# Rows of rounded products on a cleared array, issued on TensorE ahead of the first tile of a hybrid convolution, attention and PEER block

## The chip, the cores and the metric

The kernel runs on one core of one Trainium2 chip. Its time is device microseconds of that core for one execution: 997.12 us, the median of two runs (997.07 and 997.18).

## What is computed

The reference is one layer of a causal decoder block over 256 tokens of 1,024 channels, all in float32:

```
h = x + W_out( sig(g_conv) * ConformerConv(xn) + sig(g_attn) * DilatedAttn(xn) ),  xn = RMSNorm(x)
y = h + PEER(RMSNorm(h))
```

One input projection of `xn` gives the input of the convolution, the queries, keys and values of 12 heads of 64 in three dilation groups, and two gates. `PEER` scores product keys (8 heads, 2 x 128 sub-keys, the best 16), and then sums over 16,384 single-neuron experts: their activations are `gelu(u_e . x)` times a softmax gate, and the output is the sum of `act * v_e`. None of this is touched by the change: the products that it adds read an array of zeros and constants, and nobody reads what they write.

## The kernel before, in words

Weights come from HBM as tiles of 128 x 1,024 float32 (512 KB). The first 76 (`N_FRONT`) are the projections, then come 128 tiles of `u` and 128 of `v`. `raw`, `hi` and `lo` are rings of four slots. SyncE queues the loads (`load`, L387), each as soon as the slot of `raw` is free, which is when `lo` of the tile four back is made. ScalarE rounds a tile to float32r (`split_hi`, L335), which waits until TensorE is done with the slot of `hi`. GpSimd or VectorE computes the rest, raw minus hi (`split_lo`, L354). TensorE multiplies in three rounded products, hi x hi, hi x lo and lo x hi, for each block of 128 x 128 weights (`product`, L1218 for the input and `u` tiles, 256 columns each; L1527 and L1553 for the `v` tiles, 512 columns each). "Rounded product" below means such a float32r matmul; it is one instruction of the profile. A matmul on float32 operands stands in the profile as two instructions (the 27 warm-ups as 54), a float32 transpose as one.

The order on TensorE is a list written by hand (`jobs_in_order`), each job with a bank of PSUM and the waits for what it reads. It starts with 27 warm-up matmuls (`WARM_UP`, L1233: 128 columns of ones, float32, into bank 5), which wait only for `ones` (`const` at 2). Then it waits for `const` at 7 and goes to `first_tiles` (L1242 in `high_products`, L1249 in `low_products`, L1265 for the sums of squares), which work on the input before its norm is known. Their operands come from ScalarE (`xg_hi` at L481, `hi` at L335) and VectorE (`xg_lo` in `x_lo` at L738, and L748). The sums of squares are needed by ScalarE's square root, that by VectorE's reciprocal, and that by the normalised input in `norm_space`, which is first written after this point. So `norm_space` is unused until then.

`norm_space` holds 4,104 float32r values on each partition. The moving operand of a rounded product in the input stage begins 8 values (32 bytes) behind its start (`SHIFT`). Other kinds of work between the rounded products, which the prediction uses: `bias_row` (L1228), the sums over heads (L1286, two columns of `kmask`, and L1296), transposes (L1440, L1491, L1495), the gate products in float16 (L1476), and `spread_k` (L1306), which waits for VectorE's `rk_parts`.

GpSimd makes the constants at the start: `ones`, `ident`, `u_pad`, `kmask` (L434 to L440), and an affine select that puts ones on the diagonal of `ident` (L442), which takes `const` to 8.

Of the kernel before, what the change touches and what calls it, by code (L numbers as in the profile page):

```python
# [7 lines left out]
F32 = mybir.dt.float32  # L8
F32R = mybir.dt.float32r
U32 = mybir.dt.uint32  # L10
F16 = mybir.dt.float16
# [4 lines left out]
P = 128  # L16
D = 1024
T = 256
# [33 lines left out]
PICK_TILE = 60  # L52
HALF = NK // 2
GATE_SCALE = 2.0 ** 15
WARM_UP = 27
G_SHARED = N_FRONT + HALF + LEAD
TOK = 8
PAIR = 2
# [107 lines left out]
def hybrid_block(nc, x_t, front, cols, rel_bias, onehot, sub_keys, u_tiles, v_tiles, out):  # L166
    bias_row = nc.dram_tensor("bias_row", (HEADS, BW), F32, kind="Internal").ap()
    toeplitz = nc.dram_tensor("toeplitz", (HEADS, P * BW), F32, kind="Internal").ap()
    with ExitStack() as ctx:
        def sb(name, shape, dt=F32, stack=ctx):  # L170
            return stack.enter_context(nc.sbuf_tensor(name, shape, dt))

        def sem(name):
            return ctx.enter_context(nc.semaphore(name))

        bank = [ctx.enter_context(nc.psum_tensor(f"bank{i}", [P, 512], F32)) for i in range(8)]


        norm_space = sb("norm_space", [P, KB * 2 * T + SHIFT], F32R)
# [4 lines left out]
        ident = sb("ident", [P, P])  # L184
# [4 lines left out]
        def tmp(name, shape, dt=F32):  # L189
            return sb(name, shape, dt, inner)  # L190

        ones = tmp("ones", [P, P])
# [3 lines left out]
        kmask = tmp("kmask", [P, 2 * HEADS - 2])  # L196
# [77 lines left out]
        pe_step = sem("pe_step")  # L274
        act_evac, dve_evac = sem("act_evac"), sem("dve_evac")
        const = sem("const")
        squared = sem("squared")
        pair_sums = sem("pair_sums")
        normed = sem("normed")
# [422 lines left out]
        def _(dve):  # L702
# [31 lines left out]
            def x_lo(k):  # L734
# [4 lines left out]
                                         in1=xg_hi[:, i, :].bitcast(F32), op0=ALU.mult, op1=ALU.subtract)\  # L739
                   .then_inc(xlo, 1)  # L740

            dve.wait_ge(gain_in, 16)
            for k in range(XG_ACT):
                if k % 4 == 0:
# [343 lines left out]
            weights = [21] * HALVES + [25] + TC * ([13] + [35] * (PH // 2) + [25] + [13, 18, 12] * 2 + [3])  # L1088
# [109 lines left out]
        def _(pe):  # L1198
# [32 lines left out]
            pe.wait_ge(const, 2)  # L1231
            for _ in range(WARM_UP):
                pe.matmul(bank[5][:, 0:P], ones[:, :], ones[:, :], start=True, stop=True)  # L1233
            pe.wait_ge(const, 7)

            def high_products(b, n):
# [171 lines left out]
            for b_ in range(KB):  # L1408
                b = start(("attn", b_))
                units = list(range(AB * b_, AB * b_ + AB))  # L1410
                for u in units:
                    n = T_ATT + u // 8
                    if b_ == 0:
                        freed(pe, ("o", u))
                    ins = product(b[:, 0:T], n % RING, [(u % 8, u % AB)], o_hi, o_lo, n, 0, 0,
                                  first=u == units[0], last=u == units[-1])
# [16 lines left out]
            for u in range(2, HALVES):  # L1433
                step(full(T_WQ + u, ("wq", u), xg_hi, xg_lo))
                if u == 2:

                    freed(pe, ("mix", KB - 1))
                    for c in range(TC):
                        for k in range(KB):
                            ins = pe.matmul(bank[2 * c + k // 4][:, (k % 4) * P:(k % 4 + 1) * P],  # L1440
                                            resid[:, k, c * P:(c + 1) * P], ident[:, :], is_transpose=True,
                                            start=k % 4 == 0, stop=False, skip_group_check=True)
# [3 lines left out]
            for j in range(N_SC):  # L1446
                b = start(("sc", j))
                for r in range(4):
# [3 lines left out]
                                    start=r == 0, stop=True, skip_group_check=True)  # L1452
# [93 lines left out]
            for b in range(4):  # L1546
                c, cols = b // 2, slice(b % 2 * 512, b % 2 * 512 + 512)
                for j in (RING - 2, RING - 1):
# [3 lines left out]
                    for a_, v_ in ((act_hi, hi), (act_hi, lo), (act_lo, hi)):  # L1552
                        ins = pe.matmul(bank[b][:, :], a_[:, j, c * P:(c + 1) * P], v_[:, j, cols],  # L1553
                                        start=False, stop=j == RING - 1 and a_ is act_lo, skip_group_check=True)
# [73 lines left out]
```

## Time and profile before

| | us |
|---|---|
| median of two runs | 997.12 |
| the profiled execution, as timed | 997.07 |
| its span in the profile | 995.2 |
| outside the span | 1.9 |
| TensorE matmuls busy | 989.8 |
| VectorE busy | 774.9 |
| ScalarE busy | 506.8 |
| GpSimd busy | 465.3 |

Times are microseconds from the start of the span. PE is TensorE, PEld its weight loads, DVE VectorE, ACT ScalarE, POOL GpSimd, and SPq the queue of SyncE. A matmul's duration in the trace covers its way through a pipeline, and several are under way at once. What one costs in a row of many is the distance from its start to the next start, so the prediction works with starts, or with a stretch divided by its count. In a row of the windows view, "(x20)" counts each matmul that is under way somewhere in the window, so some two or three that began before it are in the count. The granted clock is a share of full speed.

### The profile page before, as it was taken

The numbers are of one execution on the slowest core, as the hardware profiler recorded it, in microseconds if no ns is written. First come the engines' busy times: TensorE is split into PE (matmuls) and PEld (weight loads), VectorE is DVE, ScalarE is ACT, GpSimd is POOL, SyncE is SP. The second block draws the span as 40 slices with busy tenths as digits, with TensorE's granted clock in tenths as the row PEclk, the third lists the DMA queues.
The fourth block names the chain that finished last, engine by engine and source line by source line (L and its number), as shares of the span: only waits on it lengthen the run. The fifth ranks groups of instructions, "written<-read, shape, count | busy, mean of one in ns | idle before, by whom it ended". The sixth has DMA issues, their size and how long they took to land.

```text
span 995.2 us, 21854 instructions
## 1 busy us (share of the span) xinstructions
PE 989.8 (99%) x7822; PEld 917.0 (92%) x7822; DVE 774.9 (78%) x1304; ACT 506.8 (51%) x789; POOL 465.3 (47%) x198
## 2 busy tenths in 40 slices
PE   9999999999999999999999999999999999999998
PEld 9998999999999999999999999888888888888887
DVE  5999784868899996097777777988888876776764
ACT  6663877544555544544444444444444445554443
POOL 3664366656689999874444444100000004344442
PEclk9999999999999999999999999999999999999999
DMA  6684445654455565555555555555554555556562
GB/s 242 211 308 150 149 148 162 212 201 149 150 197 200 171 211 188 191 176 184 177 180 174 182 172 169 185 175 170 177 180 171 182 174 190 190 189 195 186 203 90
DMA packets 52619, 181.95 MB, mean 183 GB/s; under 512 B 5943, under 2 KB 9155, under 8 KB 52452
## 3 DMA queue, kind: packets, MB, share of 16 engines
q1 hardware_dynamic: 52292, 181.16, 54.4%
q8 instruction: 25, 0.41, 0.2%
q10 hardware_dynamic: 288, 0.27, 0.1%
q14 instruction: 14, 0.11, 0.0%
HBM read 180.33 MB, written 3.43 MB: 185 GB/s over the span
## 4 chain that ended last, share of the span: by engine, by line
PE 93%; DVE 5%; ACT 1%; issue 0%; POOL 0%; ACTq 0%; DVEq 0%; POOLq 0%
PE bank L1218 50%; PE bank L1527 35%; DVE bank L798 3%; PE bank L1476 3%; PE bank L1319 1%; PE bank L1233 1%; PE bank L1451 1%; DVE lo L354 1%; PE bank L1242 1%; PE bank L1553 1%; PE bank L1335 1%; ACT hi L335 0%; PE bank L1358 0%; PE bank L1346 0%; PE bank L1249 0%
## 5 line engine op out<-in xcount | busy, mean ns | idle before, releaser
L354 POOL TENSOR_TENSOR lo<-raw,hi 128x1024 fp32r<-128x1024 f32 x184 | 462.4, 2527 | 515.9 <-ACT hi L335 515.4
L335 ACT CAST hi<-raw 128x1024 fp32r<-128x1024 f32 x332 | 348.0, 1049 | 218.0 <-PE bank L1527 186.3
L1218 PE MATMUL bank<-norm_space,hi 128*128 128x256 f32 x2624 | 452.4, 278 | 0.2 <-POOL lo L354 0.2
L1218 PEld LDWEIGHTS bank<-norm_space,hi 128*128 128x128 f32 x2624 | 396.2, 188 | 1.8 <-issue 1.2
L1218 PE MATMUL bank<-norm_space,lo 128*128 128x256 f32 x1312 | 362.8, 277 | 0.0
L1527 PE MATMUL bank<-hi,norm_space 128*128 128x512 f32 x1008 | 273.8, 391 | 0.0
L1218 PEld LDWEIGHTS bank<-norm_space,lo 128*128 128x128 f32 x1312 | 246.4, 188 | 0.0
L1527 PEld LDWEIGHTS bank<-hi,norm_space 128*128 128x128 f32 x1008 | 188.0, 188 | 38.5
L354 DVE TENSOR_TENSOR lo<-raw,hi 128x1024 fp32r<-128x1024 f32 x148 | 189.2, 1279 | 27.4 <-ACT hi L335 27.3
L1527 PE MATMUL bank<-lo,norm_space 128*128 128x512 f32 x504 | 155.5, 390 | 0.0
L1145 DVE TENSOR_TENSOR norm_space<-act,norm_space 128x256 fp32r<-128x256 f32 x128 | 111.7, 876 | 48.8 <-ACT norm_space L665 48.8
L645 ACT ACTIVATE act<-bank 128x256 f32 (+1 forms) x128 | 49.2, 384 | 187.8 <-PE bank L1218 187.8
L1527 PEld LDWEIGHTS bank<-lo,norm_space 128*128 128x128 f32 x504 | 94.6, 188 | 19.7
L1218 PE MATMUL bank<-rounded_space,hi 128*128 128x256 f32 x496 | 87.0, 280 | 0.0
L1138 DVE SCALAR_TENSOR_TENSOR act<-bank,act 128x512 f32 (+1 forms) x64 | 41.4, 686 | 51.7 <-PE bank L1476 51.7
L1126 DVE TENSOR_TENSOR ohB<-eqB,parts 128x1024 f16<-128x1024 f16 x64 | 81.4, 1272 | 0.0
L1218 PEld LDWEIGHTS bank<-rounded_space,hi 128*128 128x128 f32 x496 | 75.4, 188 | 0.9 <-issue 0.6
L1218 PE MATMUL bank<-rounded_space,lo 128*128 128x256 f32 x248 | 69.1, 278 | 0.0
L665 ACT CAST norm_space<-act 128x256 fp32r (+1 forms) x128 | 51.4, 402 | 0.1
L1218 PEld LDWEIGHTS bank<-rounded_space,lo 128*128 128x128 f32 x248 | 47.0, 190 | 0.0
L798 DVE SCALAR_TENSOR_TENSOR bank<-u_pad,prm,bank 128x256 f32<-128x256 f32 x116 | 46.3, 481 | 0.0
L1122 DVE TENSOR_TENSOR ohA<-iota_nk,keys 128x1024 f16<-128x1024 f16 x64 | 46.1, 720 | 0.0
(183 smaller groups left out, 651.5 us busy)
## 6 DMA issues: line engine op xcount, KB each, us to landing
raw<-u_tiles SPq DMA_DIRECT2D x128, 512.0 KB, 3.3
raw<-v_tiles SPq DMA_DIRECT2D x128, 512.0 KB, 3.3
raw<-front SPq DMA_DIRECT2D x76, 512.0 KB, 3.8
toeplitz<-bias_row SPq DMA_DIRECT2D x6, 384.0 KB, 7.5
bias<-toeplitz SPq DMA_DIRECT2D x12, 128.0 KB, 3.5
resid<-x_t SPq DMA_DIRECT2D x2, 512.0 KB, 4.7
qk<-sub_keys SPq DMA_DIRECT2D x1, 1024.0 KB, 8.0
y<-act SPq DMA_DIRECT2D x3, 256.0 KB, 2.0
```

Source lines behind the costliest of these rows:

```text
L335: act_e.copy(hi[:, s, :], raw[:, s, :]).then_inc(hi_ready, 1)
L354: eng.tensor_tensor(lo[:, s, :], raw[:, s, :], hi[:, s, :].bitcast(F32), ALU.subtract)\
L645: a.activation(act[:, it * 4 + (base_i + j), :], bank[4 + j % 2][:, 0:T], ACT.Gelu).then_inc(gelu_done, 1)
L665: a.copy(act_hi[:, (base_i + j) % RING, :], act[:, it * 4 + (base_i + j), :]).then_inc(a_hi, 1)
L798: dve.scalar_tensor_tensor(out=acc[:, b, :] if w == TAPS - 1 else part_sum, in0=src, scalar=wt, in1=part_sum, op0=ALU.mult, op1=ALU.add).t ...
L1122: dve.tensor_tensor(ohA[:, g % 2], every_pair(iota_nk[:, :, :], NK), at(keys[:, 0, t], NK), ALU.is_equal).then_inc(spread, 1)
L1126: dve.tensor_tensor(ohB[:, g % 2].rearrange("p a i n b -> p (a i) n b"), eqB[:, :, :, :].unsqueeze(2).broadcast_to([P, TOK // PAIR, 2, HAL ...
L1138: dve.scalar_tensor_tensor(out=av, in0=gv, scalar=1.0 / GATE_SCALE, in1=av, op0=ALU.mult, op1=ALU.mult)\
L1145: dve.tensor_tensor(act_lo[:, s, :], act[:, it * 4 + (base_i + j), :], act_hi[:, s, :].bitcast(F32), ALU.subtract).then_inc(a_lo, 1)
L1218: ins = pe.matmul(dst, w_[:, s, u * P:(u + 1) * P], x_[:, k, :], start=first and i == 0 and p_ == 0, stop=last and i == n - 1 and p_ == 2)
L1476: ins = pe.matmul(bank[6 + g][:, q * HALF:(q + 1) * HALF], ohA[:, g, q // PAIR, :, q % PAIR], ohB[:, g, q // PAIR, i, :, q % PAIR], start= ...
L1527: ins = pe.matmul(bank[2 * c + half][:, :], a_[:, j, c * P:(c + 1) * P], v_[:, j, half * 512:(half + 1) * 512], start=False, stop=False, s ...
```

## The change

`WARM_UP` goes from 27 to 20. VectorE clears the first 6 x 256 values of `norm_space` before anything else. Behind the warm-ups TensorE waits for that and for `const` at 8. Then it issues rows of rounded products that read both operands from the cleared part, all into bank 5:

- for each of eight pairs of positions (`LAYOUTS`), three times: two instances of another kind (transposes, float32 products with two columns, float32 products with 128 columns), then 11 rounded products of 256 columns;
- for each of 14 kinds of interruption: two transposes, 10 rounded products, the interruption (rounded products of other widths or positions, float16 products with 64 columns, a float32 product), 9 rounded products.

That makes 264 and 266 rounded products of 256 columns, 44 transposes, and 10 further rounded products, 11 float16 products, 17 float32 products of 128 columns and 17 of two.

```
-WARM_UP = 27
+WARM_UP = 20
+LAYOUTS = ((8, 448), (8, 192), (24, 448), (24, 192), (0, 448), (0, 192), (16, 448), (16, 192))
...
+        cleared = sem("cleared")
...
+            dve.memset(norm_space[:, 0:6 * T].bitcast(F32), 0.0).then_inc(cleared, 1)
             dve.wait_ge(gain_in, 16)
...
             for _ in range(WARM_UP):
                 pe.matmul(bank[5][:, 0:P], ones[:, :], ones[:, :], start=True, stop=True)
+            pe.wait_ge(cleared, 1)
+            pe.wait_ge(const, 8)
+
+            def rounded_products(first, apart, count, columns=T, weights=P):
+                at = first + 4 * T - apart // 4
+                for _ in range(count):
+                    pe.matmul(bank[5][0:weights, 0:columns], norm_space[:, at:at + weights],
+                              norm_space[:, first:first + columns], start=True, stop=True)
+
+            def turned(count):
+                for _ in range(count):
+                    pe.transpose(bank[5][:, 0:P], ones[:, :], ident[:, :])
+
+            def masks(count):
+                for _ in range(count):
+                    pe.matmul(bank[5][:, 0:2], ones[:, :], kmask[:, 0:2], start=True, stop=True)
+
+            def full_products(count):
+                for _ in range(count):
+                    pe.matmul(bank[5][:, 0:P], ones[:, :], ones[:, :], start=True, stop=True)
+
+            def half_products(count):
+                narrow = norm_space[:, 0:P].bitcast(F16)
+                for _ in range(count):
+                    pe.matmul(bank[5][:, 0:64], narrow[:, 0:P], narrow[:, P:P + 64], start=True, stop=True)
+
+            for first, apart in LAYOUTS:
+                for before in (turned, masks, full_products):
+                    before(2)
+                    rounded_products(first, apart, 11)
+
+            between = (lambda: rounded_products(8, 448, 1, 64), lambda: rounded_products(8, 448, 1, 128),
+                       lambda: rounded_products(8, 448, 1, 32), lambda: rounded_products(8, 448, 1, 224),
+                       lambda: rounded_products(8, 448, 1, 240), lambda: rounded_products(8, 448, 2, 128),
+                       lambda: rounded_products(8, 416, 1), lambda: rounded_products(8, 416, 1, 64),
+                       lambda: rounded_products(8, 448, 1, 512), lambda: half_products(1), lambda: half_products(2),
+                       lambda: half_products(8), lambda: full_products(1), lambda: masks(1))
+            for kick in between:
+                turned(2)
+                rounded_products(8, 448, 10)
+                kick()
+                rounded_products(8, 448, 9)
             pe.wait_ge(const, 7)
```

## Rows read from the trace of the kernel before

**Rows 1.** The page: busy time of each engine, share of the span
```profile
PE 989.8 (99%) x7822; PEld 917.0 (92%) x7822; DVE 774.9 (78%) x1304; ACT 506.8 (51%) x789; POOL 465.3 (47%) x198
```
**Rows 2.** The page: the chain that ended last, by engine
```profile
PE 93%; DVE 5%; ACT 1%; issue 0%; POOL 0%; ACTq 0%; DVEq 0%; POOLq 0%
```
**Rows 3.** The waits of PE: who was waited for, us in total, times, longest
```profile
PE bank L1233 <- POOL ones L434: 1.2, 1, 1.2
PE bank L1306 <- DVE rk_parts L900: 0.8, 1, 0.8
PE bank L1218 <- POOL lo L354: 0.2, 1, 0.2
```
**Rows 4.** Timeline, 0 to 10 us: start, duration, engine, line, what, count
```profile
1.17 8.82 PE L1233 MATMUL bank<-ones 128*128 128x128 f32 x54 [1.17 <-POOL ones L434]
...
2.00 0.29 POOL L442 TENSOR_SCALAR_AFFINE_SELECT ident<-ident 128x128 f32<-128x128 f32 x1 [0.25 <-POOL kmask L440]
...
5.79 2.07 DVE L738 SCALAR_TENSOR_TENSOR rounded_space<-resid,prm,rounded_space 128x256 fp32r<-128x256 f32 x5 [5.79 <-ACT rounded_space L481]
...
7.86 1.05 ACT L335 CAST hi<-raw 128x1024 fp32r<-128x1024 f32 x1 [0.61 <-DMA raw<-front]
...
9.74 0.49 PE L1242 MATMUL bank<-rounded_space,hi 128*128 128x256 f32 x2
```
**Rows 5.** Windows, PE alone: window, its us, busy (count), granted clock, DMA share, GB/s
```profile
2.00:6.00 4.00, 4.00 (x20) 1.00 0.90 310
7.00:9.60 2.60, 2.60 (x26) 1.00 1.02 410
259.50:422.80 163.30, 163.30 (x1443) 1.00 0.56 186
215.50:252.30 36.80, 36.80 (x315) 1.00 0.49 170
```
**Rows 6.** Timeline of PE around float32 products, two columns (L1286)
```profile
57.22 0.28 PE L1218 MATMUL bank<-norm_space,lo 128*128 128x256 f32 x1
57.34 1.40 PE L1286 MATMUL bank<-kmask,sq 128*128 128x2 f32 x12
58.60 0.48 PE L1218 MATMUL bank<-norm_space,hi 128*128 128x256 f32 x2
```
**Rows 7.** Timeline of PE around transposes (L1440; L1491 and L1495)
```profile
213.86 1.91 PE L1440 MATMUL bank<-ident,resid 128*128 128x128 f32 x16
215.52 0.48 PE L1218 MATMUL bank<-rounded_space,hi 128*128 128x256 f32 x2
215.84 0.28 PE L1218 MATMUL bank<-rounded_space,lo 128*128 128x256 f32 x1
...
423.23 0.38 PE L1495 MATMUL bank<-ident,act 128*128 128x128 f32 x2
423.37 0.49 PE L1218 MATMUL bank<-norm_space,hi 128*128 128x256 f32 x2
423.69 0.28 PE L1218 MATMUL bank<-norm_space,lo 128*128 128x256 f32 x1
```
**Rows 8.** Timeline of PE around float16 products, 64 columns (L1476)
```profile
434.35 0.66 PE L1476 MATMUL bank<-ohB,ohA 128*128 128x64 f16 x16
434.84 0.48 PE L1218 MATMUL bank<-norm_space,hi 128*128 128x256 f32 x2
435.16 0.29 PE L1218 MATMUL bank<-norm_space,lo 128*128 128x256 f32 x1
```
**Rows 9.** Timeline of PE around float32 products, 256 columns (L1265)
```profile
18.00 1.02 PE L1265 MATMUL bank<-sq,ones 128*128 128x256 f32 x4
18.67 0.60 PE L1218 MATMUL bank<-rounded_space,hi 128*128 128x256 f32 x2
19.11 0.28 PE L1218 MATMUL bank<-rounded_space,lo 128*128 128x256 f32 x1
```

## The prediction, made before the changed kernel was run

> **What bounds the kernel now.** I read the page first. TensorE is busy for 99% of the span, VectorE for 78%, the others for about half [rows 1], and the chain that ended last lies 93% on TensorE [rows 2]. So the question is how much TensorE ever waits, and the view of its waits answers it: 2.2 us in all. Of these, 1.2 us are the start, 0.8 us a wait for VectorE before L1306, and 0.2 us a wait for one `lo` tile [rows 3]. From its first warm-up to its last product TensorE is one queue that hardly ever stands still. Whatever is put into that queue is paid in full, unless it takes the place of one of those waits, and those waits are together about 1 us behind the start.
>
> Then the timeline of the start. The warm-ups run from 1.17 us and the first real product starts at 9.74 us [rows 4]. It needs `hi` of tile 0, which ScalarE makes from 7.86 for 1.05 us, to 8.91 us, and `xg_lo`, which VectorE begins at 5.79 us [rows 4]. Both are there before 9.74, so it is the end of the warm-ups that released the first product. The windows show two speeds there. From 2 to 6 us there are 20 warm-up instructions in 4.00 us (one or two of them begun before), which is 0.21 us from start to start. From 7 to 9.6 us there are 26 (two or three begun before) in 2.60 us, which is 0.11 us [rows 5]. The granted clock reads 1.00 in both rows. The beat halves all the same, as from 1.2 to 2.4 GHz, while TensorE does nothing but warm-ups.
>
> Third, what a rounded product of 256 columns costs. In the long stretch from 259.50 to 422.80 us there are 1,440 of them in 163.3 us, 0.1134 us each. From 215.50 to 252.30 us there are 312 in 36.8 us, 0.118 us each [rows 5] (three of each window's count began before it). The same instruction on the same kind of operands thus has two beats, a fast and a slow one, and holds either for tens of microseconds. Both of these stretches follow matmuls of another kind.
>
> **The change part by part.**
>
> *Warm-ups.* Seven fewer are 14 instructions, and those that go are at the fast beat: 14 x 0.112 = 1.6 us less. The probes then begin at 9.74 - 1.57 = 8.17 us. The beat has doubled before 7 us [rows 5], inside the 20 that stay, so nothing after them runs at the slow clock as long as TensorE goes on working. It does.
>
> *The waits added on TensorE.* `const` reaches 8 with the affine select, which ends at 2.29 us [rows 4]. The clearing is 1,536 values per partition on VectorE, and no row shows it. Nearest is L738, 256 values in 0.41 us (2.07 for 5) [rows 4]. Six times that is 2.5 us, from well under 1 us on the clock of the span, so it ends by about 3.5 us. The bound from below is nothing. In both cases it is ready long before 8.17 us, and VectorE has nothing to do before 5.79 us [rows 4]. I take 0.
>
> *The other kinds in the probe.* Two transposes and the step to the next product: from 423.23 to 423.37, 0.14 us [rows 7]. Two float32 products of two columns are four instructions. Twelve take 57.34 to 58.60, 1.26 us, with the last one short because the next kind follows at once [rows 6], so four take 0.37 us (0.42 if I simply take a third). Two float32 products of 128 columns are four instructions at 0.11, also 0.37 us, from the warm-ups (0.45 at most) [rows 5]. Of a float16 product: 16 in 0.49 us, 0.03 us each [rows 8].
>
> *Rounded products behind another kind.* The first two take 423.37 to 423.69, 0.32 us, and the same 0.32 us after L1440 and after L1476 [rows 7, 8]. That is 0.09 more than twice the fast beat. I allow another 0.02 us for a beat that takes a few products to settle, with 0 as its low end. Eleven products: 0.32 + 9 x 0.1134 + 0.02 = 1.36 us. After float32 products of 256 columns the first two take 0.44 us [rows 9], but the probe has none of these.
>
> *First block.* For one pair of positions: kinds 0.14 + 0.37 + 0.37 = 0.88, products 3 x 1.36 = 4.08, in all 4.96 us. Eight pairs: 39.7 us.
>
> *Second block.* Each round has transposes 0.14, ten products 0.32 + 8 x 0.1134 + 0.02 = 1.25, nine products 9 x 0.1134 = 1.02, in all 2.41 us. Fourteen: 33.7 us. The interruptions: ten rounded products of 32 to 512 columns, for which no row shows a width under 256. From below I take 0.03 us, the float16 product of 64 columns [rows 8]. From above I take a float32 product of the same width, 0.22 us for 128 columns [rows 5] and 0.34 for 256 (two instructions, four in 0.67) [rows 9]. I take 0.08 to 0.11, near the rounded product itself, and 0.23 for the one of 512 columns, 1.1 us together. The eleven float16 products are 0.33 plus three returns of 0.09, 0.6 us. One float32 product of each width with its return is 0.23 each, 0.5 us. Sum 2.2 us (1.2 to 4).
>
> *Probe in all:* 39.7 + 33.7 + 2.2 = 75.6 us. The bounds: if every product holds the slow beat, 530 x 0.0046 = 2.4 us more, and with the high ends of the interruptions (1.8) and of the float32 kinds (0.05 + 0.08 in each of eight groups, 1.0) that makes 80.8. With the low end of the interruptions and no slow start (38 rows of 0.02), it is 73.8.
>
> *Where the rounded product itself could differ.* The probe reads weights and columns from one array, and zeros. The warm-ups read both operands from `ones`, at the 0.11 us that two-column and 128-column float32 instructions of different arrays also show [rows 5, 6], so I see no price for one array. The windows of 256 columns are as in the kernel. I take the fast beat.
>
> The Trainium skill ("TensorE: Matmul & The Clock Gate", section "Back-to-back issue gap") gives the columns divided by 2.4 GHz plus about 2.5 ns, which for 256 columns is 109 ns. The trace has 113.4 and 118 ns [rows 5], so this rule would make the 530 products 2.3 us cheaper. The sum goes by the rows.
>
> *What is late next.* While TensorE works on the probe, the other engines finish what they can: four tiles rounded, `lo` of them, the squares and their sums. Then they stop, because ScalarE's next `hi` needs a slot that TensorE must free, and the square root needs TensorE's sum. From then on they stand relative to TensorE as before. The next four `raw` tiles are in, which can at most take away short waits. TensorE's waits behind the start are 1.0 us [rows 3], and VectorE's late `rk_parts` comes from its own work around 40 to 80 us, which moves along with TensorE. I take 0.1 us for this and keep 0 to 1.1. The step from the warm-ups to the first real product (0.2 us instead of 0.11) is now between equal kinds: 0.1 us less.
>
> *Total.* 997.07 - 1.57 + 75.6 - 0.1 - 0.1 = **1070.9 us**. The profiled execution (997.07) and the median (997.12) differ by 0.05, so the median of the changed kernel is forecast as 1070.9 too.
>
> **The rivals.**
>
> *The later stretches change their beat.* The kernel's own long stretches keep the beat that they fall into after an interruption. The probe shifts all that follows in time. If the 1,440 products from 259.5 us fell into the slow beat, they would cost 1,440 x 0.0046 = 6.6 us more, 1077.5 us. If only the 312 that are slow now became fast, 1.4 us less. For it: nothing in these rows says what chooses the beat. Against it: both runs of this kernel lie within 0.11 us, so what chooses it repeats, and the kernel's order between its interruptions is unchanged. Slow-beat stretches are the smaller part, so a reshuffle is more likely to cost than to give.
>
> *The probe runs at half the clock or the products collide in the one array.* If transposes broke the clock, each of the 530 products would need about twice its time, as the warm-ups do at the low level [rows 5]: 530 x 0.107 = 57 us more, 1128 us. If reading both operands from one array made a product as dear as one float32 instruction of 256 columns (0.215 us [rows 9]), the result would be the same within 3 us. Against it: 16 transposes in a row (L1440) are followed by products at 0.11 to 0.12 us [rows 5, 7]. A group of the probe has two transposes in about 1.5 us.
>
> The Trainium skill bears on the first half ("TensorE: Matmul & The Clock Gate", "Part 4: PE-mode transpose"): it says that transposes don't count as busy time for the clock. With about 5 of 76 us in transposes, that would leave the clock up here too.
>
> *The other side: the probe does not run.* Nobody reads bank 5 after it. Were the matmuls dropped when the program is built, or the queue free enough to hide them, only the warm-ups would change. The first product would then wait for `hi` of tile 0 until about 8.95 us instead of 9.74, and the time would be 996.3 us, no change. It decides on whether dead matmuls survive: the warm-ups are dead too, write the same bank, and all 54 instructions are in the trace [rows 4]. Hiding 75 us would need idle time of TensorE, and there are 2 us [rows 3].
>
> **How the numbers follow.** Forecast, 1067.5 to 1074.5 us (the probe within its bounds, waits regained up to 1.1, beats as now or nearly): 68%. Later stretches or the probe itself at a slower beat, 1074.5 to 1082: 18%. Cheaper than 1067.5, if narrow products cost nothing, stalls go and slow stretches turn fast: 7%. Half clock or colliding reads, around 1128: 5%. Not run, or the like, 996: 1%, and 1% for things unthought. The range reaches from 1067.5 to 1079, which takes in the rival at 1077.5. Two per cent of this kernel is 20 us, about what a measurement can tell from no change. Only the case where the probe does not run lies inside, so slower has 0.98, within 2% 0.015 and faster 0.005.
>
> **What would show it.** In the profile after: 40 instructions at L1233, the last before 8.2 us; the first L1242 product at about 83.7 us (8.17 + 75.6); a stretch of about 75.6 us on the new lines at granted clock 1.00 with about 660 matmuls; VectorE's clearing over before 4 us; from the first L1242 on the same sequence as now, 74 us later, ending 74 us later. The forecast is wrong if the products of the new lines stand over 0.12 us apart, if the first L1242 is not at 82 to 89 us, or if the distance to the kernel before, 74 us there, grows or shrinks by more than 2 us until the end.

## The result: 1071.07 us, and the profile of the changed kernel

| | us |
|---|---|
| before, median of 2 | 997.12 |
| changed, median of 2 (1070.76 and 1071.37) | 1071.07 |
| ratio, with its 95% interval | 1.0743 (1.0725 to 1.0760) |
| forecast | 1070.9, range 1067.5 to 1079.0 |
| the profiled execution, and its span | 1071.37, 1069.6 |

Three further executions of the same kernel on another occasion, and a fourth with a profile, gave a median of 1071.27 (1070.98 to 1072.18), against 997.02 for the kernel before on the same chip.

The page's first part and its chain, after:

```profile
PE 1064.2 (99%) x8471; PEld 991.0 (93%) x8471; DVE 776.1 (73%) x1305; ACT 506.6 (47%) x789; POOL 464.6 (43%) x198
...
PE 94%; DVE 4%; ACT 1%; issue 0%; POOL 0%; ACTq 0%; DVEq 0%; POOLq 0%
```

They answer to [rows 1] and [rows 2]. TensorE has 649 more instructions and 74.4 us more of busy time, the others have what they had. The span grew by the same 74.4 us (995.2 to 1069.6). The view of TensorE's waits, after, answers to [rows 3]:

```profile
PE bank L1236 <- POOL ones L436: 1.2, 1, 1.2
PE bank L1351 <- DVE rk_parts L903: 0.8, 1, 0.8
PE bank L1221 <- POOL lo L356: 0.2, 1, 0.2
```

These are the same three waits with the same lengths. In this execution nothing was hidden by the probe and nothing was held up by it. The timeline of TensorE and VectorE at the start, after (start, duration, engine, line; L1236 are the warm-ups, L744 the clearing, L1248 transposes, L1243 rounded products of the probe, L1252 two-column products, L1287 the first real ones):

```profile
1.15 1.34 DVE L744 MEMSET norm_space<- 128x1536 f32 x1 [1.15 <-PEq L1666]
...
1.17 6.72 PE L1236 MATMUL bank<-ones 128*128 128x128 f32 x40 [1.17 <-POOL ones L436]
...
7.73 0.38 PE L1248 MATMUL bank<-ident,ones 128*128 128x128 f32 x2
7.86 1.52 PE L1243 MATMUL bank<-norm_space 128*128 128x256 f32 x11
9.22 0.50 PE L1252 MATMUL bank<-kmask,ones 128*128 128x2 f32 x4
9.58 1.54 PE L1243 MATMUL bank<-norm_space 128*128 128x256 f32 x11
...
83.63 1.22 PE L1287 MATMUL bank<-rounded_space,hi 128*128 128x256 f32 x9
```

The clearing took 1.34 us and was over at 2.49, long before anyone needed it. Behind the first two transposes stand eleven products, which take 9.22 - 7.86 = 1.36 us from the first start to the start of the next kind. The windows of the two blocks of the probe (window, its us, busy (count), granted clock, DMA share, GB/s):

```profile
7.73:47.28 39.55, 39.55 (x347) 1.00 0.26 89
47.28:83.64 36.36, 36.36 (x322) 1.00 0.00 1
```

The granted clock is full throughout. The DMA moves almost nothing in the second window: the rings are full and everything else stands still. Further on, the long stretches that the prediction worried about:

```profile
333.90:497.20 163.30, 163.30 (x1443) 1.00 0.54 187
289.90:326.70 36.80, 36.80 (x315) 1.00 0.50 172
```

They hold the same number of products in the same time as the two in [rows 5]. In a comparison of both traces matmul by matmul, from the first real product to the last, the changed kernel takes 982.47 us against 982.03. Most of the difference, 0.38 us, lies in two places: the 72 products for the first three tiles stood 118 ns apart in place of 113.4 (the groups of 32, 16 and 16 of them took 0.19 us more), and 48 products behind the first group of float16 products did the same (0.19 us). The profiled execution is the slower of the two, and every term below is read from it.

### The profile page after: what moved, and what is told of

Read it like the earlier page. It is cut to its first block, busy times and chain, and to the rows that moved or that the text cites. A ratio compares the mean times of both kernels' runs of the same rounds, so it can differ in the third digit from the quotient of the medians.

```text
span 1069.6 us, 23154 instructions
## 1 busy us (share of the span) xinstructions
PE 1064.2 (99%) x8471; PEld 991.0 (93%) x8471; DVE 776.1 (73%) x1305; ACT 506.6 (47%) x789; POOL 464.6 (43%) x198
## 4 chain that ended last, share of the span: by engine, by line
PE 94%; DVE 4%; ACT 1%; issue 0%; POOL 0%; ACTq 0%; DVEq 0%; POOLq 0%
PE bank L1221 46%; PE bank L1572 32%; PE bank L1243 6%; DVE bank L801 3%; PE bank L1521 3%; PE bank L1364 1%; PE bank L1496 1%; PE bank L1236 1%; DVE lo L356 1%; PE bank L1287 1%; PE bank L1598 1%; PE bank L1380 0%; ACT hi L337 0%; PE bank L1248 0%; PE bank L1403 0%
## 5 line engine op out<-in xcount | busy, mean ns | idle before, releaser
L1243 PE MATMUL bank<-norm_space 128*128 128x256 f32 x540 | 72.6, 286 | 0.0
L1243 PEld LDWEIGHTS bank<-norm_space 128*128 128x128 f32 x540 | 65.8, 189 | 0.0
```

What stands on the lines that cost most here:

```text
L1243: pe.matmul(bank[5][0:weights, 0:columns], norm_space[:, at:at + weights], norm_space[:, first:first + columns], start=True, stop=True)
```

## The experiments

Each is one edit. The kernel before, timed beside them, had medians of 996.7 to 997.1 us, with single executions from 996.2 to 997.9.

**The probe without its second block.**

```
-            for kick in between:
+            for kick in ():
```

> The changed kernel without the second block of the probe (the 14 rounds around interruptions; it took 47.28 to 83.64 us there, 36.4 us). Theory, all of the probe is on the path: the first real product at 47.3 us and 36.4 us less, 1034.7 us, and, as the last row of the first block is at the fast beat, the first tiles too (0.2 us less than in the changed kernel). Rival, part of the second block was hidden beside work that other engines had to do anyway: less than 36 us comes back, and waits of TensorE appear behind the start.

Measured: 1035.80 and 1038.32 us. In the trace of the first, the first real product is at 47.30 us, as expected, and its waits are these:

```profile
PE bank L1236 <- POOL ones L436: 1.2, 1, 1.2
PE bank L1221 <- POOL lo L356: 0.8, 2, 0.7
```

The part from the first real product on took 0.96 us more than in the kernel before: 1.3 us more in the stretch with the longer wait for a `lo` tile of GpSimd (0.4 of it is some 90 more products at the slow beat), and 1.1 us given back later, where the wait for `rk_parts` is gone. Two things of the expectation failed: the first tiles ran at the slow beat although the last row was fast, and the time was 1.1 to 3.6 us too long. The rival fits the total but not the trace: the first real product came earlier by the block's full length, and VectorE, ScalarE and GpSimd were idle for the last 7 us of the probe (40 to 47 us), so a shorter probe took nothing from their head start. Why the stretch behind it was longer stays open.

**The probe without its first block.**

```
-            for first, apart in LAYOUTS:
+            for first, apart in ():
```

> The changed kernel without the first block of the probe (the eight pairs of positions; 39.55 us there, from 7.73 to 47.28 us). Without the second block the two executions were 1035.8 and 1038.3 us, 1.1 and 3.6 more than the 1034.7 that its length gave, with a wait of 0.7 us for GpSimd in the trace. Theory A, each block costs its length and the rest is scatter: 1071.2 - 39.55 = 1031.7 us, within 1 us over eleven executions. Theory B, a shorter probe gives something back (the other engines' head start or the loads stand badly to the first tiles): 1033 to 1035 us, with waits of TensorE behind the start over 1.5 us.

Measured over five executions: median 1031.8 us (1031.50, 1031.77, 1031.80, 1032.73, 1034.98); ratio to the kernel before 1.0357 (1.0343 to 1.0372). Theory A holds for the median. In the profiled execution the first real product is at 44.04 us, 39.6 earlier, and all from there on takes 982.49 us, within 0.02 us of the changed kernel. One of five was 3 us longer, like the one of 1038.32 above. Both of these have a mean granted clock of 0.998, and the other executions of the two kernels 1.000. A mean of 0.998 over some 1,035 us is some 3 to 5 us at half clock, which costs about 2 us where TensorE has work (an estimate from these numbers). So a part of the extra time may be a spell at half clock. No profile of such an execution was taken, and where the time lies is open.

**Warm-ups.**

```
-WARM_UP = 27
+WARM_UP = 20
```

> The kernel before with 20 warm-ups and nothing else. Theory: the warm-ups release the first real product at 9.74 us, and with seven fewer (1.57 us) it is released by hi of tile 0 at about 8.95 us: first product at 9.0 us, 0.7 to 0.8 us less, 996.3 us. Rival: the first product needs something later than that (other tiles, xg_lo), and what is won there is lost at a wait within the first 20 us: 997.1 us.

Measured over 11 executions: 996.44 us, against 996.75 for the kernel before; ratio 0.9997 (0.9988 to 1.0006), so no difference that can be told. The trace, though, shows the step that was forecast. The warm-ups are over 1.14 us before the first real product, which starts 0.1 us after ScalarE has made `hi` of tile 0 (7.76 + 1.04 = 8.80 us):

```profile
1.17 6.60 PE L1233 MATMUL bank<-ones 128*128 128x128 f32 x40 [1.17 <-POOL ones L434]
7.76 1.04 ACT L335 CAST hi<-raw 128x1024 fp32r<-128x1024 f32 x1 [0.46 <-DMA raw<-front]
8.91 1.30 PE L1242 MATMUL bank<-rounded_space,hi 128*128 128x256 f32 x9 [1.14 <-issue]
```

The view names no engine for this wait ("issue"); that it is `hi` is read from the times. The product came 0.83 us earlier than in the first profile of the kernel before, but everything from it on took 982.51 us in place of 982.03, 0.26 of it in the first tiles, which ran at the slow beat.

The kernel before, profiled a second time unaltered, shows the other part of why little is won:

> The kernel before unaltered, once more. Theory A, beats repeat: slow stretches at 24, 58, 76, 87, 91, 103, 113 to 134, 142, 148 and 215 us as in the first profile, 982.0 us from the first real product to the last. Theory B, they are drawn anew: other stretches, up to 2 us of difference in that distance.

```profile
1.17 8.05 PE L1233 MATMUL bank<-ones 128*128 128x128 f32 x54 [1.17 <-POOL ones L434]
9.00 1.28 PE L1242 MATMUL bank<-rounded_space,hi 128*128 128x256 f32 x9
```

Here the same 54 instructions needed 8.05 us, not 8.82 [rows 4], and the execution 996.34 us. From the first real product to the last it took 982.05 us against 982.03, with two neighbouring stretches (18 to 56 us) shifted by 0.2 us against each other: theory A, nearly. What differs is how many of the warm-up instructions ran at half clock: 24 of 54 in the first profile, 16 in this one. Over all traces with warm-ups it was 14 to 28 instructions, and each costs 0.213 us in place of 0.112. So the warm-ups end sooner or later from one execution to the next: with 20 of them, the next instruction started anywhere from 7.30 to 8.63 us.

**No warm-ups, with the probe.**

```
-WARM_UP = 20
+WARM_UP = 0
```

> The changed kernel with no warm-ups. The probe begins when the clearing is done (2.5 us in the changed kernel) and at half clock. Theory A, the probe's mixture raises the clock as the warm-ups did (5.3 us of work at the slow clock): 2.5 + 75.9 + 2.6 = first real product at 81.1 us, 2.5 us less, 1068.5 us. Theory B, transposes and narrow products hold the clock down: the products stay over 0.21 us apart for tens of microseconds, 1080 to 1130 us.

```profile
2.58 0.66 PE L1248 MATMUL bank<-ident,ones 128*128 128x128 f32 x2 [2.58 <-DVE norm_space L744]
2.90 2.69 PE L1243 MATMUL bank<-norm_space 128*128 128x256 f32 x11
5.39 0.84 PE L1252 MATMUL bank<-kmask,ones 128*128 128x2 f32 x4
6.09 2.57 PE L1243 MATMUL bank<-norm_space 128*128 128x256 f32 x11
8.50 0.61 PE L1256 MATMUL bank<-ones 128*128 128x128 f32 x4
...
81.21 0.63 PE L1287 MATMUL bank<-rounded_space,hi 128*128 128x256 f32 x4
```

Measured 1069.18 and 1069.43 us. Eleven products take 2.49 us (2.90 to 5.39) instead of 1.36, then 2.41, then the usual. The first real product is at 81.21, forecast 81.1; the time is 0.7 and 0.9 us above the forecast. Theory A: the probe's own mixture raises the clock.

**Transposes in place of the rounded products of the first block.**

```
-                    rounded_products(first, apart, 11)
+                    turned(11)
```

> The changed kernel with transposes in place of the rounded products of the first block: 264 transposes, with the two float32 products of each kind still between them. Theory A, transposes hold the clock up as other work does: 109 ns each, the first block takes 24 x 11 x 0.109 + 8 x 0.98 = 36.6 us in place of 39.5, about 1068 us. Theory B (the Trainium skill, TensorE: Matmul & The Clock Gate, Part 4: PE-mode transpose, says that they do not count as busy time): the granted clock falls to half within the block, and 264 x 0.105 = up to 28 us more, some 1080 to 1096 us.

```profile
12.00:20.00 8.00, 8.00 (x77) 1.00 0.81 279
20.00:40.00 20.00, 20.00 (x187) 1.00 0.01 2
```

Measured 1068.93 us (one execution). With some 184 instructions in 20 us (187 less those begun before), 0.109 us each, and a granted clock of 1.00 for the whole block, theory B is out for these float32 transposes: they are some 280 of the 344 instructions and 31 of the 37 us, and TensorE kept its 2.4 GHz. The other 64 are instructions of float32 products. They alone don't explain it, because the same 64 stand between the narrow products of the next experiment, and there the clock falls. The clock was up before the block began, so this shows that such transposes hold it, not that they would raise it. Where the Trainium skill ("TensorE: Matmul & The Clock Gate", "Part 4: PE-mode transpose") and this measurement differ, the measurement decides.

**64 columns in place of 256.**

```
-                    rounded_products(first, apart, 11)
+                    rounded_products(first, apart, 11, 64)
...
-                rounded_products(8, 448, 10)
+                rounded_products(8, 448, 10, 64)
...
-                rounded_products(8, 448, 9)
+                rounded_products(8, 448, 9, 64)
```

> The changed kernel with 64 columns in place of 256 in all 530 rounded products of the probe's rows. Theory A: a rounded product costs no less than the load of its own weights, about 113 ns, whatever its width (in the changed kernel a narrow interruption and the product after it took 228 ns together, as much as two wide ones): the probe stays 75.5 us long within 1.5 us, 1071 us. Theory B, the columns set the price, as for the float16 products of 64 columns at 30 ns: 530 x 0.084 = 44 us less, 1027 us.

Measured 1131.33 and 1131.39 us, 60 us more than with four times as many columns. The timeline and the windows:

```profile
8.08 0.38 PE L1248 MATMUL bank<-ident,ones 128*128 128x128 f32 x2
8.21 1.39 PE L1243 MATMUL bank<-norm_space 128*128 128x64 f32 x11
9.44 0.59 PE L1252 MATMUL bank<-kmask,ones 128*128 128x2 f32 x4
...
141.68 3.55 PE L1287 MATMUL bank<-rounded_space,hi 128*128 128x256 f32 x15
```

```profile
7.90:12.70 4.80, 4.80 (x47) 1.00 0.69 255
14.00:20.00 6.00, 6.00 (x30) 0.50 0.88 280
20.00:40.00 20.00, 20.00 (x97) 0.50 0.02 6
...
120.00:141.00 21.00, 21.00 (x110) 0.50 0.00 0
144.00:160.00 16.00, 16.00 (x128) 0.94 0.14 45
```

Both theories get an answer. At full clock eleven narrow products took 9.44 - 8.21 = 1.23 us, 0.112 us each, and they don't pay the 0.09 us that wide ones pay behind another kind, so a row of eleven takes 1.23 in place of 1.36 us. A product of 64 columns costs nearly what one of 256 costs (0.1134 or 0.118), so theory A is right about the price at one clock. Consistent with this, the weight load is what they share; it was not measured by itself. But after three such rows the granted clock fell to one half (1.2 GHz), while the view calls TensorE busy all the time, and stayed there until the 256-column products of the first tiles had run for some 4 us (the window from 144 us reads 0.94). At half clock they stand 0.213 us apart. The half clock was a rival of the prediction, with its price for the whole probe at 57 us. The changed kernel, whose narrow products come singly or in pairs between wide ones, does not meet it. The wide products read the same zeros at full clock, so the values are not the reason. What in the narrow rows lets the clock fall is not told by this run.

**Other positions.**

```
-LAYOUTS = ((8, 448), (8, 192), (24, 448), (24, 192), (0, 448), (0, 192), (16, 448), (16, 192))
+LAYOUTS = ((0, 416), (8, 416), (0, 160), (8, 160), (16, 416), (24, 416), (8, 448), (0, 448))
```

> The changed kernel with other positions in the first block: in order (moving, weights) begin at 0,32 / 32,0 / 0,32 / 32,0 / 0,32 / 32,0 / 32,32 / 0,0 bytes beside a multiple of 64. Theory A (position, both operands must be aligned or one is enough): rows of the last pair (0,0) are all fast, of 32,32 some slow, and the mixed ones show which operand counts: if the moving one, all rows of 0,32 are fast and some of 32,0 slow; if the weights, the other way round. Theory B (time and history alone): slow and fast rows in all pairs, without order. The time is 1071 us within 1.2 us by either.

Measured 1072.40 and 1072.79 us, above the 1.2 us that both theories allowed. In the trace the probe began 0.9 us later than in the changed kernel (28 slow warm-up instructions) and was 0.4 us longer. Timeline of this kernel, the transposes with which each pair of positions begins:

```profile
13.63 0.38 PE L1248 MATMUL bank<-ident,ones 128*128 128x128 f32 x2
...
18.62 0.38 PE L1248 MATMUL bank<-ident,ones 128*128 128x128 f32 x2
...
38.65 0.38 PE L1248 MATMUL bank<-ident,ones 128*128 128x128 f32 x2
...
43.62 0.38 PE L1248 MATMUL bank<-ident,ones 128*128 128x128 f32 x2
...
48.54 0.38 PE L1248 MATMUL bank<-ident,ones 128*128 128x128 f32 x2
```

A mixed pair takes 4.99 us (13.63 to 18.62), and the pair at (0, 448) 4.92 us. In all 18 rows whose two operands stand differently to a multiple of 64 bytes, the products are mostly 115 to 122 ns apart (up to 127) in a pattern that neither the fast nor the slow beat has, and none settles at 113. Only where both stand alike is there a fast beat. None of the forms of theory A fits the mixed rows, since neither operand alone decides. Its forecast for the last two pairs held: the rows at (8, 448) were slow twice and fast once, the three at (0, 448) fast. In the changed kernel the aligned rows of the first block all came last, from 27.7 us on, when the DMA was at rest (share 0.00, and 0.51 before), so the DMA could have been what made the others slow. Here the rows at (8, 448) ran with the DMA at rest (0.01 from 38.7 us on), and two of three were slow.

**The kernel before, moved by 32 bytes.**

```
-SHIFT = 8
-ACT_SHIFT = 24
+SHIFT = 16
+ACT_SHIFT = 32
```

> The kernel before, without any probe, with all float32r arrays moved by 32 bytes (SHIFT 8 to 16, ACT_SHIFT 24 to 32). In the changed kernel the products of the probe whose two operands begin at a multiple of 64 bytes (first 0 or 16) ran at the fast beat of 113.4 ns in all 12 rows, and those that begin 32 bytes beside one (first 8 or 24) at the slow beat of 118 ns in about half. Theory A, the position decides whether the slow beat can be held: the kernel's operands all begin 32 bytes beside a multiple of 64, so moved by 32 they never hold it; some 800 products at 118 ns in the kernel before become 113.4, 3.7 us less, about 993.4 us, and the 312 products behind L1440 stand 113.4 ns apart. Theory B, the beat comes from what went before and the probe's positions are a coincidence: slow stretches are still there, others than before perhaps, 995 to 1001 us.

Measured over 11 executions: 998.25 us, ratio 1.0014 (1.0005 to 1.0023): slightly slower, not 3.7 us faster. Theory A is refuted by the trace as well. Its windows:

```profile
152.99:211.40 58.41, 58.41 (x505) 1.00 0.58 200
216.80:253.00 36.20, 36.20 (x309) 1.00 0.48 169
261.00:420.00 159.00, 159.00 (x1405) 1.00 0.53 185
```

The second, the 312 products behind L1440, is at 0.118 us as before. The first holds the 504 products of the stretch ahead of it, now 0.116 apart on average; in the kernel before the same stretch began at 152.99 too and took 57.25 us, 0.1136 each, so 1.3 us were lost here. The 0.116 is a mean of the two beats: start by start, some 20 products at the fast beat are followed by some 245 at 0.118, some 190 at 0.1134 and some 45 at 0.118. So a long stretch can change its beat with nothing else between its products. Aligned operands hold the slow beat as well. That all 12 aligned rows of the probe were fast did not carry over to the kernel.

**What stands just ahead of the first tiles.**

```
                 kick()
                 rounded_products(8, 448, 9)
+            turned(2)
+            rounded_products(0, 448, 9)
```

> The changed kernel with two transposes and nine rounded products at the position 0, 448 behind the probe, 1.25 us more. Theory A, the first tiles take over the beat of the row before them: after this row at the fast beat the 72 products of the first tiles stand 113.4 ns apart (118 in the changed kernel), 0.3 us less; in all 1072.0 us. Theory B, the first tiles' own operands (32 bytes beside a multiple of 64) or the time choose the beat: they run at 118 ns as in the changed kernel, 1072.3 us. The trace tells them apart, not the time.

```
                 rounded_products(8, 448, 9)
+            full_products(2)
```

> The changed kernel with two float32 products of 128 columns behind the probe, just ahead of the first real product, 0.5 us more, about 1071.5 us. After a row at the fast beat and after one at the slow beat alike, the first tiles ran at 118 ns when rounded products went straight over into them, and at 113.4 ns in the kernel before, where float32 products stood just ahead. Theory A, the kind just ahead decides: the first tiles run at 113.4 ns, 0.2 us less over their 72 products. Theory B, the length of time or the operands decide: they stay at 118 ns.

Measured 1072.38 and 1073.12 us for the first, 1071.79 us for the second. Windows of 7.50 us from just behind the first real product, in this order for the first and for the second kernel:

```profile
84.60:92.10 7.50, 7.50 (x66) 1.00 0.01 2
```

```profile
84.50:92.00 7.50, 7.50 (x69) 1.00 0.01 2
```

After a row at the fast beat the first tiles still ran at 118 ns (66 under way in the window, as in the changed kernel). After two float32 products they ran at 113.4 ns (69). In the changed kernel's form rounded products go over into rounded products without a break, after a slow row there and after fast rows in the first experiment and here, and all three times the tiles are slow. So the beat is not handed on. An interruption just ahead gave the fast beat here and in both profiles of the kernel before. It is no rule: in the kernel moved by 32 bytes the same tiles stand behind the same warm-ups and are slow, with 20 warm-ups they stand behind a wait of 1.1 us and are slow, and within the probe three of the eight rows behind float32 products of 128 columns were slow.

**The changed kernel again.**

> The changed kernel unaltered, once more. In the runs so far 16 to 28 of the 40 warm-up instructions were at the slow clock (0.213 us) and the rest at 0.112 us, so the probe began anywhere from 7.5 to 8.6 us. Theory A, this moment of the rise is the main scatter between executions and the rest repeats: the probe is 75.9 us long within 0.1 us with the same rows fast and slow (229 products at 116 to 119 ns), the part from the first real product on within 0.2 us, and the times lie within 1.5 us of each other around 1071 us. Theory B, the beats are drawn anew in each execution: another count of slow products (150 to 350) and a probe of 75.5 to 76.5 us.

Measured 1070.98 to 1072.18 us, median 1071.27. The probe took 75.90 us (75.91 before), with 226 products at 116 to 119 ns against 229, and all from the first real product on 982.62 us against 982.47. It began at 8.40 us in place of 7.73, with 25 slow warm-up instructions in place of 19. Theory A holds for all that it forecast. But the equal sums hide a difference. From 106 to 158 us more products stood at the slow beat than in the first profile (191 of one stretch of 216, which had 2 there), 1.1 us more in all, and the view of TensorE's waits lacks one line:

```profile
PE bank L1236 <- POOL ones L436: 1.2, 1, 1.2
PE bank L1221 <- POOL lo L356: 0.2, 1, 0.2
```

The wait for `rk_parts` is gone. VectorE had them ready 73.65 and 73.64 us after the first real product, and the products that read them start at 73.80 and 73.81, whether TensorE was early for them (first profile) or not (this one). So the slow beat ahead of that wait cost nothing, up to about 1 us.

## Why the prediction was right, step by step

The forecast was 1070.9 us and the median is 1071.07. The two executions lie 0.6 us apart, and the profiled one, from which the terms are read, is 0.5 above the forecast, so a part of the closeness is luck. Not every term was that good; some errors cancelled.

- *TensorE is one queue that never waits, and all of the probe is paid.* Right. The waits are the same three, and without the first block the kernel gives its length back (median 1031.8 us for the forecast 1031.7). Without the second block the first real product came 36.3 us earlier, but the two executions were 1.1 and 3.6 us longer than that gives, 0.5 us of it behind the first real product in the one that was profiled, so the lengths add up to about 1 us and no better.
- *Warm-ups.* The 14 instructions were sized rightly, but the probe was to begin at 8.17 us and began at 7.73. The clock rose after 19 slow instructions, not 24. This term is not fixed: it was 7.3 to 8.6 us in the traces with 20 warm-ups. The prediction took one execution's clock rise for the kernel's. Here it took 0.44 us off. The two executions of the changed kernel differ by 0.6 us, which this alone could make, though only one of them was profiled.
- *First block*, 39.7 us: 39.55.
- *Second block*, 33.7 + 2.2 = 35.9 us: 36.36. Beside the warm-ups this is the term that was most off inside the probe's part. The interruptions were priced at 0.08 to 0.11 us where they are narrow, and the narrow rows show that 64 columns cost 0.112 us; that makes about 0.1 to 0.15 of the 0.46 us. The rest is the slow beat, which 229 of the probe's intervals have, and which the prediction left out of its value and kept in its upper end (2.4 us for all, so about 1.0 for these). In the first block the allowances for settling covered it.
- *First real product* at 83.7 us: 83.64.
- *Behind it*, forecast 0.1 us less: 0.44 us more, 0.38 of it from two places at the slow beat. The 0.1 us of waits regained did not come in the first profile; in the second 1.1 us were regained and lost again to the slow beat. The rival that later stretches change their beat is thus right in kind and far off in size: 0.4 us where 6.6 was its price for the longest one. That it can strike harder is shown by the move of 32 bytes, which cost the stretch of 504 products 1.3 us.
- *The half clock.* It did not come, and the reason given against it was right for transposes: rows of them hold the clock up. Reading both operands from one array did not cost anything either: the products stood at the same two beats as the kernel's own. What the prediction did not see is that rows of narrow products bring the half clock about, within 5 us and for as long as they last.
- *The probe not run.* Out; 649 instructions more are in the trace.

What chooses between the two beats stays open. Equal position of both operands to a multiple of 64 bytes was needed for the fast one in the probe, but it is not enough. For a given build the choice mostly repeats: most stretches were the same in two traces each of both kernels, and what differed lay in the first 160 us, where some 190 products of one stretch changed over.

## What to carry to other kernels

In a kernel whose TensorE waits for 1 us in all, added matmuls cost their start-to-start distance, and the sum over kinds read from the trace came within 0.3 us over 76. A rounded product with its own weights costs about 0.112 us with 64 columns and 0.1134 or 0.118 with 256, so narrowing it wins next to nothing, and rows of narrow ones can cost the full clock besides. Time lost ahead of a wait for another engine is lost only beyond that wait's length, so read the waits behind a stretch before you price it. Before a microsecond is credited to an edit at the start, count the slow warm-up instructions in more than one trace, because that count alone moved the end of the warm-ups by 1.3 us.

## What was not expected of the hardware

- Rows of 64-column float32r products, 0.112 us apart, with a few transposes and float32 products between them, brought the granted clock from 1.00 to 0.50 about 5 us after they began, with TensorE shown as busy for 100% of the time, and held it there as long as they lasted, some 130 us.
- Float32 transposes at 0.109 us each, with 64 instructions of float32 products among 344, kept it at 1.00 for 37 us.
- Two float32r operands that stand differently to a multiple of 64 bytes gave 115 to 122 ns in nearly all intervals of 18 rows, without ever settling at the fast beat of 113.4.
- The moment at which the clock rises varied from 14 to 28 slow warm-up instructions between executions of kernels that start alike.
